# GLA norm and gate products on row and column groups, and the chunk products ordered by width

## The reference

```python
h, gate_res = ada_modulate(x, c, norm_g, ada_w, ada_b)
gq, gk, gv, glr, sq, sk, sv, gate = _split(h @ in_w, ODD_SIZES)      # glr has rank 16
log_a = log_sigmoid((glr @ gate_w + gate_b)) / 16.0                  # [256, 512]
# per chunk of 64 positions, 4 heads of 128 keys and 256 values
att = where(mask, einsum('bnthk,bnshk->bnhts', q_dec, k_inv), 0.0)
o   = einsum('bnhts,bnshv->bnthv', att, vf) + q_dec @ state
yc  = rmsnorm(o, gla_norm_g)                                         # over the 256 values of a head
y   = concatenate([yc, yd]) * silu(gate)
```

## Time and profile before

| | us |
|---|---|
| median of 3 runs | 1023.59 (1022.42 to 1023.84) |
| the profiled execution | 1022.46 |
| its span in the profile | 1020.6 |
| TensorE busy / VectorE / ScalarE / GpSimd | 978.7 / 723.5 / 514.5 / 41.0 |

### The profile page before, as it was taken

The page is one execution under the profiler, slowest core; times in us unless marked ns, Lnnn a source line. Parts: engine busy times, 40 slices in busy tenths (PEclk is TensorE's granted clock), DMA queues, the critical chain, the costliest instruction groups (busy, mean ns, idle before and its releaser), DMA issues.

```text
span 1020.6 us, 19346 instructions
## 1 busy us (share of the span) xinstructions
PE 978.7 (96%) x8087; PEld 959.7 (94%) x8087; DVE 723.5 (71%) x1027; ACT 514.5 (50%) x755; POOL 41.0 (4%) x67
## 2 busy tenths in 40 slices
PE   6999999999999999999999999998997999999998
PEld 6999999989999999999999999998997999999997
DVE  4777967777646845767999788697966666465555
ACT  4554355456544455644754564556374454444442
POOL 2100000000000012401000000000000000000000
PEclk9999999999999999999999999999997999999999
DMA  9986576647764966478467667785323356466621
GB/s 367 365 294 240 188 267 248 250 165 244 249 207 145 329 228 242 149 260 279 164 245 256 245 249 252 243 276 173 130 84 124 125 165 223 149 239 202 200 102 42
DMA packets 138959, 219.57 MB, mean 215 GB/s; under 512 B 7161, under 2 KB 110922, under 8 KB 138872
## 3 DMA queue, kind: packets, MB, share of 16 engines
q1 hardware_dynamic: 136576, 213.94, 60.6%
q10 hardware_dynamic: 1336, 2.64, 0.7%
q0 software_dynamic: 960, 1.76, 0.6%
HBM read 217.25 MB, written 1.05 MB: 214 GB/s over the span
## 4 chain that ended last, share of the span: by engine, by line
PE 82%; DVE 10%; issue 3%; ACT 3%; DMA 2%; ACTq 0%; DVEq 0%
PE pw L558 60%; PE pacc L558 22%; DVE WL L1561 2%; DMA ring<-in_ada_w 1%; ACT AR L1104 1%; DVE ACC L1577 1%; DVE hl L1660 1%; DVE SQT L1655 1%; DMA cst<-in_consts 1%; ACT WH L1104 1%; DVE AR L1577 0%; ACT hh L1104 0%; PE pw L950 0%; DVE AR L1777 0%; ACT YH L1104 0%
## 5 line engine op out<-in xcount | busy, mean ns | idle before, releaser
L1104 ACT ACTIVATE WH<-ring 128x1024 fp32r<-128x1024 f32 x288 | 301.8, 1055 | 262.3 <-PE pw L558 180.0
L558 PE MATMUL pw<-hh,WH 128*128 128x256 f32 x1408 | 403.6, 287 | 10.2 <-DVE WL L1561 6.2
L1561 DVE TENSOR_TENSOR WL<-ring,WH 128x1024 fp32r<-128x1024 f32 x288 | 343.9, 1222 | 77.0 <-ACT WH L1104 76.5
L558 PE MATMUL pw<-hl,WH 128*128 128x256 f32 x1408 | 398.2, 283 | 0.0
L558 PE MATMUL pw<-hh,WL 128*128 128x256 f32 x1408 | 398.2, 283 | 0.0
L558 PEld LDWEIGHTS pw<-hh,WH 128*128 128x128 f32 x1408 | 269.8, 192 | 16.2 <-issue 14.0
L558 PEld LDWEIGHTS pw<-hl,WH 128*128 128x128 f32 x1408 | 270.0, 192 | 0.0
L558 PEld LDWEIGHTS pw<-hh,WL 128*128 128x128 f32 x1408 | 269.9, 192 | 0.0
L558 PE MATMUL pacc<-YH,WH 128*128 128x256 f32 x672 | 192.3, 286 | 3.5 <-issue 2.5
L558 PE MATMUL pacc<-YL,WH 128*128 128x256 f32 x672 | 190.6, 284 | 0.0
L558 PE MATMUL pacc<-YH,WL 128*128 128x256 f32 x672 | 190.6, 284 | 0.0
(11 more groups left out here) (249 smaller groups left out, 815.1 us busy)
## 6 DMA issues: line engine op xcount, KB each, us to landing
ring<-in_w_mod SPq DMA_DIRECT2D x72, 512.0 KB, 5.8
ring<-in_odd_in_w SPq DMA_DIRECT2D x56, 512.0 KB, 6.9
ring<-in_ada_w SPq DMA_DIRECT2D x48, 512.0 KB, 8.1
ring<-in_ffn_w_gate SPq DMA_DIRECT2D x44, 512.0 KB, 4.8
ring<-in_ffn_w_up SPq DMA_DIRECT2D x44, 512.0 KB, 5.4
ring<-in_ffn_w_down SPq DMA_DIRECT2D x44, 512.0 KB, 4.6
ring<-in_even_in_w SPq DMA_DIRECT2D x40, 512.0 KB, 7.2
ring<-in_even_out_w SPq DMA_DIRECT2D x16, 512.0 KB, 5.5
```

The lines of the kernel that those rows point to most:

```text
L558: return eng.matmul(o, a, b, start=start, stop=stop, skip_group_check=True)
L1104: return eng.activation(dst, src, func, **kw)
L1561: tt(WL[:, i % NL, :], slot(half_of(i)), WH[:, i % NH, :].bitcast(F32), SUB).then_inc(s_lo, 1)
```

## The change

- `GLW` and `GLT` (rank-16 operands) exist twice: on partitions 0 to 15 and 32 to 47, `GLW` with half of the columns each. GpSimd issues two loads, ScalarE copies `gl` twice (new semaphore `s_glt`). `lw0` and `lw1` are opened together, and their four products alternate between the two row groups and the two banks.
- `at`: within a block the four 128-column products come first, then the four 64-column ones.
- `gs`: eight products of 32 columns by 256 positions; head j goes to column group j, so partitions 32j to 32j+31 hold its sums for all positions. Before, 16 products with the squares as weights and 64 columns of ones.
- `rsqrt` works on 128x256 in `SQT` in place of 128x8 in `RS`.
- `gr`: one row of the root (partition 64q + 32m) is spread by a product with a row of ones, two heads at a time into two banks, `gr0` and `gr1`, which are both held over og6. The second pair waits for VectorE's reading of the first (`s_gra`).
- VectorE's loop waits for each product (`gr00` to `gr11`) on its own.

```diff
-        GLW = AR[0:16, 19840:20352]
+        GLW = [AR[32 * q:32 * q + 16, 19840:20096] for q in range(2)]
...
-        GLT = AR[0:16, 4096:4352]
+        GLT = [AR[32 * q:32 * q + 16, 4096:4352] for q in range(2)]
...
             p.wait_ge(*gone["gl"])
-            p.wait_ge(d_glw, 16)
-            for q in range(2):
-                pb = open_(f"lw{q}", (s_dmin, 2 * q + 2))
-                for m in range(2):
-                    h = 2 * q + m
-                    last = mm(pb[:, m * T:m * T + T], GLW[:, h * P:h * P + P], GLT)
-                close(last, f"lw{q}")
+            p.wait_ge(s_glt, 1)
+            p.wait_ge(d_glw, 32)
+            lws = [open_(f"lw{q}", (s_dmin, 2 * q + 2)) for q in range(2)]
+            for m in range(2):
+                for q in range(2):
+                    last = mm(lws[q][:, m * T:m * T + T], GLW[q][:, m * P:m * P + P], GLT[q])
+                    if m == 1:
+                        close(last, f"lw{q}")
...
                     mm(pb[:, h * P:h * P + P], T2[:, t0:t0 + P], GQ[:, t0:t0 + P])
+                for h in range(4):
+                    t0 = h * T + blk * P
                     last = mm(pb[0:64, h * P + 64:h * P + P], T3[:, t0:t0 + 64], GQ[:, t0 + 64:t0 + P])
...
             pb = open_("gs")
-            for n in range(8):
-                c = 2 * (n // 2)
-                stats(pb[:, 64 * c:64 * c + 128], ones[:, 0:64], n, 8 + n, n == 0, n % 2 == 1)
+            p.wait_ge(s_sq, 16)
+            for e in range(2):
+                for j in range(4):
+                    mm(pb[32 * j:32 * j + 32, 0:T], ones[:, 0:32], SQT[:, 2 * j + e, :], e == 0, e == 1).then_inc(s_sqr, 1)
             full["gs"] = (s_sqr, 16)
             cols_T(L_ODD, f"og{next(gates)}")
+
+            grs = [open_(f"gr{m}", None, True) for m in range(2)]
+            p.wait_ge(s_r, 3)
             for q in range(2):
-                pb = open_(f"gr{q}")
-                p.wait_ge(s_r, 3)
-                for c in range(4):
-                    last = mm(pb[:, c * P:c * P + P], RS[:, 4 * q + c:4 * q + c + 1].to_broadcast([P, P]), ident)
-                close(last, f"gr{q}")
+                if q == 1:
+                    p.wait_ge(s_gra, 2)
+                for m in range(2):
+                    r = slice(64 * q + 32 * m, 64 * q + 32 * m + 1)
+                    close(mm(grs[m][:, q * T:q * T + T], ones[r, :], SQT[r, 0, :]), f"gr{q}{m}")
+                if q == 1:
+                    back("gr0")
+                    back("gr1")
                 cols_T(L_ODD, f"og{next(gates)}")
...
-                    evac("gl", GLT, src=pw[place["gl"]][0:16, 0:T])
+                    s.wait_ge(*full["gl"])
+                    act(GLT[0], pw[place["gl"]][0:16, 0:T]).then_inc(s_glt, 1)
+                    act(GLT[1], pw[place["gl"]][0:16, 0:T]).then_inc(s_bank[place["gl"]], 1)
...
-            rsqrt(RS[:, 0:8], pw[place["gs"]][:, 0:512:64], 1.0 / 256, RS[:, 8:16], RS[:, 16:24], "gs")
+            rsqrt(SQT[:, 0, :], pw[place["gs"]][:, 0:T], 1.0 / 256, SQT[:, 1, :], SQT[:, 2, :], "gs")
...
-                pb = pw[place[f"gr{q}"]]
-                v.wait_ge(*full[f"gr{q}"])
                 for m in range(2):
+                    v.wait_ge(*full[f"gr{q}{m}"])
                     for n in (4 * q + 2 * m, 4 * q + 2 * m + 1):
                         a = stt(out=YC[:, n, :], in0=YC[:, n, :], scalar=col("gla_norm_g", n),
-                                in1=pb[:, m * T:m * T + T], op0=MUL, op1=MUL)
-                        if n % 4 < 3:
+                                in1=pw[place[f"gr{m}"]][:, q * T:q * T + T], op0=MUL, op1=MUL)
+                        if n % 2 == 0:
                             v.wait_ge(*v.step(a))
+                        elif q == 0:
+                            a.then_inc(s_gra, 1)
+                            v.wait_ge(s_gra, m + 1)
                         else:
-                            a.then_inc(s_bank[place[f"gr{q}"]], 1)
-                            v.wait_ge(*gone[f"gr{q}"])
+                            a.then_inc(s_bank[place[f"gr{m}"]], 1)
+                            v.wait_ge(*gone[f"gr{m}"])
...
-            eng.dma_start(GLW, I["gla_gate_w"][0]).then_inc(d_glw, 16)
+            for q in range(2):
+                eng.dma_start(GLW[q], I["gla_gate_w"][0, :, q * T:q * T + T]).then_inc(d_glw, 16)
```

More of the change, by code:

```diff
@@ L351, in build @@
         s_chk = sem("s_chk")
+        s_gra = sem("s_gra")
+        s_glt = sem("s_glt")
         s_silu = sem("s_silu")
```

## The result

| | before | after |
|---|---|---|
| median, first comparison (4 runs each) | 1023.72 | 1017.65 |
| ratio, with its 95% interval | | 0.994 (0.9928 to 0.9953) |
| median of all runs of the study | 1023.59 (73 runs) | 1018.56 (10 runs) |
| second comparison, ratio | | 0.9947 (0.9931 to 0.9963) |
| the profiled execution / its span | 1022.46 / 1020.6 | 1018.89 / 1016.8 |

A forecast was written before the change was run, and what follows sets the result against it. TensorE was taken to bound the kernel, busy 978.7 of 1020.6 us, unless it then waits for VectorE's WL pieces. Gains of 0.2 + 2.0 + 2.3 = 4.5 us gave 1019.1 us, range 1016.8 to 1021.8.

The forecast's parts named there:

- lw: Low-rank gate: a wait before gv0 takes back most of the saving; 0.2 us gained, between 0 and 0.3.
- The link that I had counted as worth "0.24 at most": Gate's chain: a WH piece that waited 0.64 us for TensorE moves earlier and releases VectorE; 0.24 us at most.
- at: Chunk products ordered by width: six of eight width changes go, narrow records run faster; 2.0 us, between 1.3 and 2.2.
- gs: Sums of squares on four column groups: TensorE free about 2.4 us earlier, its part ending 2.55 before VectorE's old start.
- The roots: VectorE's rsqrt: 11 instructions on 256 columns take 4.6 us in all, 2.8 us more than before.
- `gr` and og7: Root spreading up to og7: og7 starts 2.3 us earlier, TensorE waiting there about 1.1 to 1.6 us.
- The sum: Whole kernel: 0.2 + 2.0 + 2.3 = 4.5 us gained, passing to the end; 1019.1 us.
- rival B: Whole kernel: no wait takes anything back, 6.8 us gained, 1016.8 us; chance 0.08.
- A: Edited stages: narrow records cost as wide ones, rsqrt at its upper bound; 2.9 us gained, 1020.7 us; chance 0.17.
- C: After the edits: all but 1 us lost at a wait not hanging on TensorE; 1022.6 us; chance 0.07.
- D: At gr and the wait before og7: the granted clock falls, costing 5.1 us; 1024.2 us; chance 0.06.
- The example near 626 us: Around 626 us TensorE waited over 2 us and the clock stayed at 1.00; cited against a clock loss.

The follow-up runs named there:

- second comparison: The changed kernel run again without further edits, against the kernel before: median 1018.69 us over 6 runs, ratio 0.9947.
- e7: The changed kernel with VectorE cutting the WL pieces of qk3's turn before that turn's two ada halves; ratio to before 0.9936.
- e8: The changed kernel with both VectorE reorderings (og6, qk3) and all wide at products of both blocks before all narrow ones; median 1016.29 us, ratio to before 0.9926.
- e3: The kernel before with only the gs, rsqrt, gr and VectorE loop parts of the change; ratio 0.9957.
- e1: The kernel before with only the low-rank gate on two row groups; ratio 1.0005.
- e4: The kernel before, unchanged, run as an experiment of its own: median 1023.94 us over 11 runs, ratio 1.0003.
- e6: The changed kernel with VectorE cutting og6's two WL pieces before its two ada halves; ratio to before 0.9931.
- e12: e8 plus eight unused products ahead of each of TensorE's waits near 136 and 628 us; median 1014.5 us, ratio to before 0.9918.
- e9: The changed kernel without the alternation: gs and lw do both products of a group one after the other; one run, 1019.61 us.

## Why the prediction was right

Point by point, in its order:

- **`lw`**: forecast 0.2, between 0 and 0.3; traces 0.25 and 0.25. Both halves of the argument held: the two row groups do run side by side (0.86 of the allowed 0.96; the first round of 0.32 us and the way out of 0.30 are as long as before), and gv0's wait takes back 0.6. `e7` shows that VectorE's order was the reason. The link that I had counted as worth "0.24 at most" is what was left.
- **`at`**: forecast 2.0, between 1.3 and 2.2; 2.02. Both terms were there: fewer changes of width, and narrow records faster than wide ones, 0.058 us from start to start in a row of their kind where wide ones take 0.112. Together that is 0.34 us for each way into the narrow width and back, and six of these went; `e8` takes out one more and gains 0.34 again.
- **`gs`**: forecast 2.4 for TensorE and 2.55 for VectorE's start; 2.40 for TensorE. VectorE starts 1.42 us behind the last main product (312.42 to 313.84), where it was 3.85: 2.43 earlier, 0.12 less than forecast. TensorE's part was sized right: from the last main product to the end of the last record 1.28 us, forecast 0.2 + 0.64 + 0.44 (which is 314.73, not 314.75). The sum had nothing for the 0.14 us from that end to VectorE's start.
- **The roots**: forecast 4.6 us for 11 instructions; 4.56, with the two tensor_scalars at 0.42 and 0.29 and the rest at 0.42 or 0.43.
- **`gr` and og7**: forecast 2.3 with a wait of 1.1 to 1.6; 2.27 (2.28 alone) with 1.18. The idle time of 2.48 us did take up the roots.
- **The sum**: 4.5 forecast, 4.54 up to og7. The median of the first comparison lies 1.5 us beyond that, and the forecast's 4.5 lies just short of its interval (4.8 to 7.4 us). It fell into the range, but the range reached down to rival B. The step that was short is "All later work hangs on TensorE and VectorE in turn; [...] so I let the gain pass to the end": 0.5 us more came later in the first trace. 0.33 of it, also in `e3`, is a wait of VectorE for 0.46 us ahead of an `ada` half near 550 us that is gone. The 0.20 near 475 us varies among traces: against that of before it was +0.29 in `e1` and +0.35 in the unchanged kernel of `e4`. With the trace of `e4` in place of that of before, the whole gain from `lw` to the end is 5.7 and not 5.0 us, 0.3 of it at the lowered clock near 780 us. So the traces give 5.0 to 5.7, and the 5.3 at equal clock lies within. What medians show beyond that goes with the rarer low clocks of the changed kernels, a term that the prediction did not have; how the edits bring it stays open.
- **The rivals**: By the number alone, B's 1016.8 lies nearer to the first median of 1017.65 than the forecast's 1019.1. The traces decide: B is out by `e1` and the wait ahead of og7. A's sizes are out by the rows. C is out, nothing was given back. D I had as a loss of 5.1 us, with 0.06. The clock does fall where I put it, in two of five traces, but the loss is 1.5 us; a clock below 1.00 between 225 and 345 us was one of my signs of being wrong, and it came in these two executions. The example near 626 us that spoke against it in the trace of before was a draw, since the clock falls there in 4 of the 13 traces without a filling. One execution's row of the clock is not a rule.

The sentence of the Trainium skill, page "TensorEngine Tiling (Array Packing)", section "Key Properties", that different tiles load and multiply in parallel, agrees with these traces: two row groups start 0.01 us apart and `lw` takes 1.06 instead of 1.92 us. The Trainium skill's page "TensorE: Matmul & The Clock Gate", section "What happens when you issue a matmul", says that a weight load's time goes with its columns. The prediction's estimate by that alone was 2.2 us for `at`; 2.02 was measured.

## What to carry to other kernels

Cost a saving on the bound engine up to the next place where that engine needs something from another, and ask what starts that other engine's chain: a chain that does not begin with the shortened work gives the saving back, as gv0 did. Then look what stands ahead of the needed piece on the late engine; moving two unurgent instructions behind it gave another 0.82 and 0.57 us by the traces (`e6`, `e7`). Behind a wait of 1 to 2 us the clock was lowered in some runs, which cost 1.2 to 1.5 us more. Read medians together with each run's mean clock. A wait that can't be removed may be filled with spare products at no cost (`e12`); that this keeps the clock up is not shown.

## What the runs showed of the hardware

- A product on a group of rows or columns overlaps with those of the other groups in both orders tried: 16 records of 128x256 on four column groups in 1.07 us alternating, 1.09 with two of the same group in succession (`e9`).
- A float32 record with 64 weight columns and 64 streamed costs 0.058 us from start to start in a run of its kind (eight in 0.68 from the first start to the last end), against 0.112 for one of 128; alternating two and two they cost 0.17 on average. Each way into the narrow width and back costs 0.34 us over staying in one.
- Single-row products (1x256 on 1x128) go at the pace of those of 16 rows, 0.32 us for the first round and 0.31 for the second with the way out: four records, two by two, in 0.70 us, and eight records of 16 rows in 1.13.
- The granted clock fell or stayed behind the same wait from one execution to the next: behind 1.8 us near 137 us (lowered in 6 of 11 traces), 2.1 near 628 us (4 of 13), and 1.2 us of waiting right after two mode changes ahead of og7 (2 of 5). Each time it was at 1.2 GHz for 3.4 us and 1.2 to 1.5 us were lost. Near 780 us it was at 1.2 GHz for 3.4, 6.8 or 10.2 us.
